# Gated linear attention on Trainium2: loads and weight splits moved ahead around the state scan

## The chip, the core and the metric

The kernel runs on one core of one Trainium2 chip. The metric is the device time of one execution in microseconds, median of several runs. Lower is better.

## What is computed

Two transformer-like blocks on a sequence of 1024 tokens of width 1024 (256 context tokens beside it), all in float32. The change lies in the first block, in its gated linear attention, which runs over the sequence in chunks and in both directions:

```python
def step(S, inp):                       # one chunk of q, k, v and log decay
    b = cumsum(ac)
    S_new = exp(b[-1]) * S + einsum('bhjd,bhjv->bhdv', kc * exp(b[-1] - b), vc)
    scores = einsum('bhid,bhjd,bhijd->bhij', qc, kc, decay)
    o = einsum('bhij,bhjv->bhiv', scores, vc) + einsum('bhid,bhdv->bhiv', qc * exp(b), S)
    return S_new, o
...
oc, s_f, s_b = gla_bidir(qc, kc, vc, laf_c, lab_c, 0, 0, with_output=False)   # context
ox, _, _ = gla_bidir(q, k, v, la_f, la_b, s_f, s_b, True)                     # sequence
```

Beside it the same input projection gives `uB`, of which moving averages over 2, 4, 8 and 16 tokens are taken (`multiscale_pool`), and the gates. All of it is multiplied by weights that the kernel streams from HBM.

## The kernel before, in words

Every weight tile (128 x 1024) is loaded into one of two raw buffers `w_raw`, and GpSimd (POOL) splits it into a high and a low part (`split`, L838: `w_hi` at L840, `w_lo` at L843). TensorE (PE) makes a tile's product as 24 matmuls a unit of 512 tokens: high by high, low by high, high by low (`pe_unit`, L478). POOL may overwrite a split buffer when the tile after its last user has begun (semaphore `w_begun`); PE waits for the split (`w_split`); SyncE (SP) loads the next raw tile when the split before it in that buffer is done (`weight`).

Around the change the program has three stages, separated by the semaphore `phase`, which PE, ScalarE (ACT) and VectorE (DVE) each raise:

- **Chunk preparation** ends with phase 6: decayed keys `kt_d`, values `vt_d`, within-chunk scores `pt_d` and decayed queries `qi_d` of the ten chunks (eight of the sequence, two of the context, numbers `NCX` and `NCX + 1`) are stored to HBM.
- **State scan**, phase 6 to 9. PE alternates a weight tile (T_S to T_S + 9, that is 55 to 64) with eight matmuls `s_products` (L2777) that multiply a chunk's keys and values; DVE updates the state with them (`s_update`, L1983). Steps 0 to 9 run backward over all ten chunks, and their states are stored to `sb_d`; steps 10 and 11 run forward over the two context chunks and have no weight tile of their own. ACT loads each step's keys and values into one of two buffers (`s_load`, L1169 and L1170), when the products two steps earlier are done. Meanwhile POOL and SP work on the moving averages: SP loads the 16 halves of `uB` (`u_load`) and a 2 MB table `inv_sb` (semaphore `tab_in`), POOL averages them (`averages(n)`), SP stores them (`u_store`).
- **Output**, phase 9 to 12. For each of the eight chunks PE makes eight matmuls for the state (L2796) and 72 for the output (L2808 to L2811); SP loads five tiles a chunk (`f_load`: keys, values, scores, queries; `f_load_states`: the backward state), three chunks ahead, into three buffers `F_BUFS`, and between them moves the last averages. ACT copies the outputs, and the pool stage follows after phase 12.

The order of POOL's work in the scan is written out by hand: in step n it splits tile T_S + 1 + n and then makes `averages(n)`, all behind the waits for phase 6 and for the table.

```python
            pool.wait_ge(phase, 6)
            ...
            pool.wait_ge(tab_in, 64)
            ...
            for n in range(16):
                t = T_S + 1 + n
                if t <= T_POOL:
                    pool.wait_ge(w_begun, t)
                    split(t % 2, t + 1, 16 * (t // 2) + 16)
                averages(n)
```

Of the kernel before, what the change touches and what calls it, by code (L numbers as in the profile page):

```python
# [22 lines left out]
P = 128  # L23
# [5 lines left out]
H = 512  # L29
EPS = 1e-6  # L30
HEADS, DK, DV = 4, 128, 256
CH = 128
NC = TA // CH
# [62 lines left out]
def build(nc, modt, modw, cond, crow, cols, mats, tabs, hmask, inv, sgb, xT, ctxT, ctx2T, wall, wup, sgw, bias,  # L96
# [7 lines left out]
    with ctx:  # L104
        def sem(name):
            return ctx.enter_context(nc.semaphore(name))
# [6 lines left out]
        def at(name, shape, offset, dt=F32):  # L113

            n = 4
            for s in shape[1:]:
                n *= s
            n = (n + 31) // 32 * 32
            assert offset % 32 == 0 and offset + n <= nc.sbuf_usable_end, (name, offset + n)
            return nc.alloc_sbuf_tensor_at(name, shape, dt, offset=offset), offset + n  # L120
# [127 lines left out]

        skb, a = at("skb", [P, 2, H], stage_end)
        svt, a = at("svt", [P, 2, 1024], a)  # L250
        stb, a = at("stb", [P, 2, HEADS, DV], a)
        s_end = a


        F_BUFS, U_BUFS = 3, 4
        gla_arena = arena + 33 * 1024
        oall, _ = at("oall", [P, 8, T], gla_arena)
        a = arena + 77 * 1024
        fpt, fqi, fkt, fvt, fsb = [], [], [], [], []
        for n in range(F_BUFS):  # L260
            for tiles_of, shape in ((fpt, [P, HEADS, CH]), (fqi, [P, 2, HEADS, CH]), (fkt, [P, H]),
                                    (fvt, [P, 1024]), (fsb, [P, HEADS, DV])):
                each, a = at(f"f{n}_{len(shape)}_{shape[1]}_{a}", shape, a)
                tiles_of.append(each)
        assert a >= s_end
        stf, _ = at("stf", [P, 2, HEADS, DV], arena + 169 * 1024)
        up, a = at("up", [P, U_BUFS, H + 2 * PAD], a)
        sums, a = at("sums", [P, 2, H + 2 * PAD], a)
# [24 lines left out]
        p_ktr = sem("p_ktr")  # L293
        p_kt = sem("p_kt")
        s_in = [sem("s_in0"), sem("s_in1")]
        s_out = [sem("s_out0"), sem("s_out1")]
        s_mm = sem("s_mm")
        s_upd = sem("s_upd")
# [342 lines left out]
        def _(sp):  # L641
# [109 lines left out]
                sp.dma_start(fqi[n].rearrange("p a h n -> p (a h n)"), qi_d[c]).then_inc(f_in[n], 16)  # L751

            def f_load_states(c):
                n = c % F_BUFS
                sp.dma_start(fsb[n].rearrange("p h n -> p (h n)"), sb_d[c]).then_inc(f_in[n], 16)

# [4 lines left out]
            for s in range(8):  # L761
                weight(T_S + 3 + s)
                u_store(s)
            sp.wait_ge(phase, 9)
            for c in range(F_BUFS):
                f_load(c)
                f_load_states(c)
            for c in range(NCX):
# [68 lines left out]
        def _(pool):  # L837
# [20 lines left out]
            with pool.Fori(1, HALVES) as i:  # L858
                for b in range(2):
                    pool.wait_ge(w_high, i * 2 + (b + 2))  # L860
                    nc.gpsimd.tensor_tensor(w_lo[:, b, :], w_raw[:, b, :], w_hi[:, b, :],
                                            ALU.subtract).then_inc(w_split, 1)
            split_pairs(HALVES, (T_S + 1) // 2)


            pool.wait_ge(phase, 6)
            for n in range(U_BUFS):
# [29 lines left out]
                  .then_inc(u_d, 1)  # L897

            for n in range(16):
                t = T_S + 1 + n  # L900
                if t <= T_POOL:
                    pool.wait_ge(w_begun, t)
                    split(t % 2, t + 1, 16 * (t // 2) + 16)
                averages(n)
            split_pairs(T_POOL // 2 + 1, NT // 2)
            pool.wait_ge(w_begun, NT - 1)
# [33 lines left out]
        def _(act):  # L940
# [244 lines left out]
                    s_step(i * 2 + b, b, i * -2 + (NC - 1 - b), (i * -2 + (NC - 2 - b), 1), i)  # L1185
            s_step(NC - 2, 0, 1, (0, 1), NC // 2 - 1)
            s_step(NC - 1, 1, 0, (NCX, 0), NC // 2 - 1)
            s_step(NC, 0, None, (NCX + 1, 0))
            for b in range(2):
                act.wait_ge(s_out[b], 16 * (NC // 2 + 1))  # L1190
            for b in range(2):
# [1431 lines left out]
        def _(pe):  # L2623
# [146 lines left out]
                p_keys(p)  # L2770
            pe.drain().then_inc(phase, 1)

            def s_products(n, b, loads):
                pe.wait_ge(s_in[b], loads)
                pe.wait_ge(s_upd, n + 1)
                for h in range(HEADS):
                    mm = pe.matmul(g[:, 2 * b + h // 2, DV * (h % 2):DV * (h % 2) + DV],  # L2777
                                   skb[:, b, DK * h:DK * h + DK], svt[:, b, DV * h:DV * h + DV],
                                   start=True, stop=True)
                mm.then_inc(s_mm, 1)  # L2780

            with pe.Fori(0, NC // 2) as i:
                for b in range(2):
                    pe_tile(pe, T_ZA + 3 * NC + b, i, 2, 4)
                    s_products(i * 2 + b, b, i * 32 + 32)
            for b in range(2):
                s_products(NC + b, b, 32 * (NC // 2 + 1))
            end_phase(pe, 3)

            for c in range(NCX):  # L2790
                b, n = c % 2, c % F_BUFS
                pe.wait_ge(f_in[n], 80 * (c // F_BUFS + 1))
                if c >= 2:
                    pe.wait_ge(f_upd, c)
                for h in range(HEADS):
# [7 lines left out]
                for h in range(HEADS):  # L2803
                    for v in range(2):
                        bank = pb[h // 2] if b == 0 else g[:, 4 + h // 2, :]
                        o = bank[:, DV * (h % 2) + CH * v:DV * (h % 2) + CH * v + CH]
                        f = slice(DV * h + CH * v, DV * h + CH * v + CH)
                        pe.matmul(o, fvt[n][:, f], fpt[n][:, h, :], start=True, stop=False)  # L2808
                        pe.matmul(o, stf[:, b, h, CH * v:CH * v + CH], fqi[n][:, 0, h, :], start=False,
                                  stop=False)  # L2810
                        mm = pe.matmul(o, fsb[n][:, h, CH * v:CH * v + CH], fqi[n][:, 1, h, :],  # L2811
                                       start=False, stop=True)
                mm.then_inc(f_omm, 1)
            end_phase(pe, 4)
# [462 lines left out]
```

## Time and profile before

| | |
|---|---|
| runs | 2685.05, 2674.70, 2686.24 us; median 2685.05 us |
| the profiled execution | 2682.14 us, span 2680.4 us |
| granted TensorE clock, mean | 0.962 of full speed |
| busy: PE, DVE, POOL, ACT | 2496.2, 1518.1, 1062.3, 731.1 us |
| state scan (phase 6 to 9) | 704.9 to 852.1 us from the span's start |
| output (first loads to last matmul) | 852.1 to 922 us |

PE is busy for 93% of the span. A change can shorten the run only where it removes idle time of PE, time at the lower clock, or matmuls. The span is read in the order of time: an engine's rows give the start of a group, its length, and in brackets the idle time before it with what ended it.

### The profile page before, as it was taken

To read this page: it belongs to the slowest core of one execution; us is meant where nothing else is said; L and a number is where in the kernel's file an instruction comes from. 1 tells how busy PE (TensorE), PEld (TensorE's weight loads), DVE (VectorE), ACT (ScalarE), POOL (GpSimd) and SP (SyncE) were. 2 spreads that over 40 slices of the span, in tenths; PEclk is the share of its full clock that TensorE was granted. 3 is DMA by queue.
4 is the path that set the end of the run, shared out by engine and by line. 5 is a ranking of instruction groups with operands and counts; after the bars stand their busy time and mean duration, and the time that the engine had idled before them with its cause. 6 is when DMAs were issued, how large, how long until landed. Compare 5 with 4: busy or idle time off the path is not lost.

```text
span 2680.4 us, 33036 instructions
## 1 busy us (share of the span) xinstructions
PE 2496.2 (93%) x12008; PEld 2044.2 (76%) x12008; DVE 1518.1 (57%) x2193; ACT 731.1 (27%) x1244; POOL 1062.3 (40%) x493
## 2 busy tenths in 40 slices
PE   8999999999897979999986999899799999999997
PEld 4888788888686857877774888678578888888885
DVE  5796157877411367446796544475864444444446
ACT  4411334444200254223232444342211111111112
POOL 2344333443465524457541111024554444444444
PEclk9999999999898989999997799989899999999998
DMA  9576455444566842434311222421211111111111
GB/s 354 184 256 242 151 162 162 139 157 142 193 226 220 310 145 81 140 102 142 107 42 60 71 77 74 150 88 61 64 55 48 48 47 47 47 47 47 47 47 71
DMA packets 131233, 325.25 MB, mean 121 GB/s; under 512 B 11568, under 2 KB 59248, under 8 KB 125616
## 3 DMA queue, kind: packets, MB, share of 16 engines
q1 hardware_dynamic: 91232, 215.63, 24.4%
q10 hardware_dynamic: 39888, 108.08, 11.4%
q8 instruction: 74, 1.21, 0.2%
q14 instruction: 39, 0.32, 0.0%
HBM read 248.57 MB, written 70.39 MB: 119 GB/s over the span
## 4 chain that ended last, share of the span: by engine, by line
PE 50%; DVE 8%; issue 3%; ACT 1%; DMA 1%; POOL 0%; DVEq 0%; SPq 0%; POOLq 0%; ACTq 0%
PE pb L478 36%; PE g L2979 6%; PE g L3052 2%; PE pb L2979 1%; DVE zcs L2249 1%; PE g L3032 1%; PE g L2960 1%; DVE f_spare L2458 1%; PE g L2839 1%; DMA kept_in<-cs_d 1%; PE g L2958 0%; DVE ml L2465 0%; DVE xl L2161 0%; DVE hl L2528 0%; DVE cb L2507 0%
## 5 line engine op out<-in xcount | busy, mean ns | idle before, releaser
L840 POOL TENSOR_TENSOR w_hi<-w_raw,one 128x1024 fp32r<-128x1024 f32 x191 | 402.3, 2106 | 1450.4 <-PE pb L478 1051.7
L843 POOL TENSOR_TENSOR w_lo<-w_raw,w_hi 128x1024 fp32r<-128x1024 f32 x191 | 517.4, 2709 | 15.0
L478 PE MATMUL pb<-xh,w_hi 128*128 128x512 f32 (+1 forms) x1224 | 476.3, 389 | 30.8 <-POOL w_lo L843 12.9
L478 PE MATMUL pb<-xh,w_lo 128*128 128x512 f32 (+1 forms) x1224 | 468.1, 382 | 0.0
L478 PE MATMUL pb<-xl,w_hi 128*128 128x512 f32 (+1 forms) x1224 | 467.9, 382 | 0.0
L478 PEld LDWEIGHTS pb<-xh,w_hi 128*128 128x128 f32 x1224 | 233.7, 191 | 79.6 <-POOL w_lo L843 14.1
L478 PE MATMUL pb<-mh,w_hi 128*128 128x512 f32 x704 | 279.1, 397 | 15.9 <-DVE ml L2465 7.3
L478 PE MATMUL pb<-mh,w_lo 128*128 128x512 f32 x704 | 276.4, 393 | 0.0
L478 PE MATMUL pb<-ml,w_hi 128*128 128x512 f32 x704 | 276.1, 392 | 0.0
L478 PEld LDWEIGHTS pb<-xl,w_hi 128*128 128x128 f32 x1224 | 233.2, 190 | 44.5
L478 PEld LDWEIGHTS pb<-xh,w_lo 128*128 128x128 f32 x1224 | 233.9, 191 | 42.9 <-issue 0.7
L478 PEld LDWEIGHTS pb<-mh,w_hi 128*128 128x128 f32 x704 | 133.5, 190 | 50.2 <-ACT mh L1605 11.7
L2551 DVE SCALAR_TENSOR_TENSOR x<-pb,modx,x 128x512 f32<-128x512 f32 x160 | 119.1, 749 | 89.1 <-PE pb L478 89.1
L478 PEld LDWEIGHTS pb<-ml,w_hi 128*128 128x128 f32 x704 | 133.7, 190 | 28.3
L478 PEld LDWEIGHTS pb<-mh,w_lo 128*128 128x128 f32 x704 | 133.9, 190 | 27.7 <-issue 0.5
L2505 DVE TENSOR_SCALAR cb<-gp,col 128x1024 f32<-128x1024 f32 x22 | 43.7, 1984 | 189.9 <-ACT gp L1645 187.4
L478 PE MATMUL pb<-hh,w_hi 128*128 128x512 f32 x352 | 138.8, 394 | 12.3 <-DVE x L2551 11.3
L478 PE MATMUL pb<-hl,w_hi 128*128 128x512 f32 x352 | 137.1, 389 | 0.0
L478 PE MATMUL pb<-hh,w_lo 128*128 128x512 f32 x352 | 137.1, 389 | 0.0
L1645 ACT ACTIVATE gp<-pb 128x512 f32<-128x512 f32 x40 | 24.0, 599 | 375.7 <-PE pb L478 375.7
L973 ACT ACTIVATE stage<-pb 128x512 f32<-128x512 f32 x80 | 47.5, 595 | 279.8 <-PE pb L478 261.3
L478 PE MATMUL pb<-bh,w_hi 128*128 128x512 f32 x256 | 102.7, 401 | 8.4 <-DVE bl L2108 4.7
(410 smaller groups left out, 4635.1 us busy)
## 6 DMA issues: line engine op xcount, KB each, us to landing
w_raw<-in_wall SPq DMA_DIRECT2D x190, 512.0 KB, 3.6
mod_later<-in_modw SPq DMA_DIRECT2D x28, 1024.0 KB, 6.4
proj_d<-stage ACTq DMA_DIRECT2D x40, 512.0 KB, 2.7
at_bias<-in_bias SPq DMA_DIRECT2D x64, 192.0 KB, 2.5
mod_raw<-in_modt SPq DMA_DIRECT2D x8, 1024.0 KB, 11.0
w_raw<-in_wall ACTq DMA_DIRECT2D x15, 512.0 KB, 7.0
svt<-vt_d ACTq DMA_DIRECT2D x12, 512.0 KB, 4.8
vc<-proj_d SPq DMA_DIRECT2D x10, 512.0 KB, 6.1
```

What stands on the lines that cost most here:

```text
L478: mm = pe.matmul(pb[bank][:, 0:n], w[:, b, wc:wc + P], x[:, k, tokens], start=(count == 0), stop=(count == total - 1))
L840: nc.gpsimd.tensor_tensor(w_hi[:, b, :], w_raw[:, b, :], one[:, 0:1].to_broadcast([P, 1024]), ALU.mult).then_inc(w_high, 1)
L843: nc.gpsimd.tensor_tensor(w_lo[:, b, :], w_raw[:, b, :], w_hi[:, b, :], ALU.subtract).then_inc(w_split, 1)
L973: act.activation(rows[:, b, lo:hi], pb[u % 2][:, 0:hi - lo], ACT.Copy, scale=scale)\
L2249: nc.vector.scalar_tensor_tensor(zcs[:, t, :], hpad[:, t, bass.ds(tap, T)], col[:, bass.ds(tap + (cw + TAPS * t), 1)], zcs[:, t, :], ALU.m ...
L2458: nc.vector.scalar_tensor_tensor(f_spare[:, 4 + k % 3, :], x2[:, k, half_of(n)], gain[:, 0, k:k + 1], f_spare[:, 2 + n, :], ALU.mult, ALU. ...
L2505: v = nc.vector.tensor_scalar(cb[:, kt, :], gp[:, kt, 0:T], w, None, ALU.mult)
L2551: nc.vector.scalar_tensor_tensor(x2[:, m, half], pb[u % 2][:, :], modx[:, 64 + m:65 + m], x2[:, m, half], ALU.mult, ALU.add).then_inc(bank ...
L2839: mm = pe.matmul(g[:, u, :], mean_v, osq[:, v, H * u:H * u + H], start=(v == 0), stop=(v == 1))
L2960: pe.matmul(g[:, s % 2, 0:HL], low, local(keys[rows, :]), start=False, stop=True)
L2979: mm = pe.matmul(dst[:, 0:n], w[:, t0 % 2, at_k:at_k + P], x[:, k, tokens], start=(begun and k == kts[0] and w is w_hi and x is xhi), stop ...
L3052: mm = pe.matmul(g[:, 4, 64 * j:64 * j + 64], ptr[:, s % 2, P * c:P * c + P], v, start=(c == 0), stop=(c == 4))
```

## The change

1. POOL splits tile T_S + 1 before it waits for phase 6, and from then on is one tile ahead: in step n of the averages it splits T_S + 2 + n.
2. The last scan step's keys and values get buffers of their own (`skx`, `svx`, semaphore `s_last`). SP loads them after the fourth store of averages in the scan; ACT's `s_step(NC, ...)`, which loaded them, is removed.
3. At the same place SP loads four of the five tiles of the first output chunk. The fifth, the backward state, is not loaded: PE reads it from the scan's own buffer `stb[:, 1]`, and waits for 64 counts instead of 80 on that buffer's semaphore. At phase 9 SP loads two chunks instead of three.
4. The tiles move in SBUF so that output buffer 0 and `skx`, `svx` share no space with the scan's.

```diff
-        stb, a = at("stb", [P, 2, HEADS, DV], a)
+        stb, a = at("stb", [P, 2, HEADS, DV], a + 3 * 1024)
...
-        a = arena + 77 * 1024
+        a = s_end
         for n in range(F_BUFS):
+            if n == 1:
+                f_end, a = a, arena + 77 * 1024
...
+        skx, a = at("skx", [P, H], f_end)
+        svx, a = at("svx", [P, 1024], a)
...
             def f_load_states(c):
+                if c == 0:
+                    return
...
             for s in range(8):
                 weight(T_S + 3 + s)
                 u_store(s)
+                if s == 3:
+                    sp.dma_start(skx[:, :], kt_d[NCX + 1][:, 0:H]).then_inc(s_last, 16)
+                    sp.dma_start(svx[:, :], vt_d[NCX + 1]).then_inc(s_last, 16)
+                    f_load(0)
             sp.wait_ge(phase, 9)
-            for c in range(F_BUFS):
+            for c in range(1, F_BUFS):
                 f_load(c)
                 f_load_states(c)
...
+            def split_next(t):
+                pool.wait_ge(w_begun, t)
+                split(t % 2, t + 1, 16 * (t // 2) + 16)
+
             split_pairs(HALVES, (T_S + 1) // 2)
-
+            split_next(T_S + 1)
 
             pool.wait_ge(phase, 6)
...
             for n in range(16):
-                t = T_S + 1 + n
-                if t <= T_POOL:
-                    pool.wait_ge(w_begun, t)
-                    split(t % 2, t + 1, 16 * (t // 2) + 16)
+                if T_S + 2 + n <= T_POOL:
+                    split_next(T_S + 2 + n)
                 averages(n)
...
-            s_step(NC, 0, None, (NCX + 1, 0))
...
-            for b in range(2):
-                s_products(NC + b, b, 32 * (NC // 2 + 1))
+            pe.wait_ge(s_in[0], 32 * (NC // 2 + 1))
+            s_products(NC, 0, skb[:, 0], svt[:, 0])
+            pe.wait_ge(s_last, 32)
+            s_products(NC + 1, 1, skx, svx)
             end_phase(pe, 3)
...
-                pe.wait_ge(f_in[n], 80 * (c // F_BUFS + 1))
+                pe.wait_ge(f_in[n], 80 * (c // F_BUFS + 1) - (16 if n == 0 else 0))
...
-                        mm = pe.matmul(o, fsb[n][:, h, CH * v:CH * v + CH], fqi[n][:, 1, h, :],
+                        before = fsb[n] if c else stb[:, 1]
+                        mm = pe.matmul(o, before[:, h, CH * v:CH * v + CH], fqi[n][:, 1, h, :],
```

How the order on two engines changes. On POOL, at the start of the scan, before (`up` are the buffers of the averages, `sums` their partial sums; the first split here is tile 56):

```order
L869 MEMSET up 128x8 [waits phase]
L869 MEMSET up 128x8 x3
L840 TENSOR_TENSOR w_hi<-w_raw,one 128x1024 [waits w_begun,w_in0,tab_in,u_s]
L843 TENSOR_TENSOR w_lo<-w_raw,w_hi 128x1024 [waits w_high]
L887 TENSOR_TENSOR sums<-up 128x527 [waits u_d,u_in0]
L894 TENSOR_TENSOR sums<-sums,inv_sb 128x512 [waits u_s]
L896 TENSOR_TENSOR up<-sums,up 128x512 [waits u_s]
L840 TENSOR_TENSOR w_hi<-w_raw,one 128x1024 [waits w_in1,w_begun]
L843 TENSOR_TENSOR w_lo<-w_raw,w_hi 128x1024 [waits w_high]
```

and with the change:

```order
L851 TENSOR_TENSOR w_hi<-w_raw,one 128x1024 [waits w_in0,w_begun]
L854 TENSOR_TENSOR w_lo<-w_raw,w_hi 128x1024 [waits w_high]
L884 MEMSET up 128x8 [waits phase]
L884 MEMSET up 128x8 x3
L851 TENSOR_TENSOR w_hi<-w_raw,one 128x1024 [waits w_begun,w_in1,tab_in,u_s]
L854 TENSOR_TENSOR w_lo<-w_raw,w_hi 128x1024 [waits w_high]
L902 TENSOR_TENSOR sums<-up 128x527 [waits u_d,u_in0]
L909 TENSOR_TENSOR sums<-sums,inv_sb 128x512 [waits u_s]
L911 TENSOR_TENSOR up<-sums,up 128x512 [waits u_s]
```

The split of tile 56 now stands in front of the wait for the phase, and the split that waits for the table (`tab_in`) is that of tile 57.

On SP, in the middle of the scan with the change (before, the row of the second `w_raw` followed directly on the first `up`):

```order
L739 DMA d_d<-up 128x512 [waits u_d]
L733 DMA up<-proj_d 128x520 [waits u_out2]
L772 DMA skx<-kt_d 128x512
L773 DMA svx<-vt_d 128x1024
L753 DMA f_2_512_167616_114<-kt_d 128x512
L754 DMA f_2_1024_169664_115<-vt_d 128x1024
L755 DMA f_3_4_161472_112<-pt_d 128x512
L756 DMA f_4_2_163520_113<-qi_d 128x1024
L682 DMA w_raw<-in_wall 128x1024 [waits w_split]
L739 DMA d_d<-up 128x512 [waits u_d]
```

Six loads (`f_...` are output buffer 0's tiles) are put between the fourth store of averages and the load of weight tile 62, and the five loads that stood first behind the wait for phase 9 are gone from there.

## Rows read from the trace of the kernel before

**Rows 1.** The page's first line: the span.

```profile
span 2680.4 us, 33036 instructions
```

**Rows 2.** Waits of PE from 690 to 930: us, times, longest.

```profile
PE pb L478 <- POOL w_lo L843: 12.0, 1, 12.0
PE g L2796 <- DMA f<-sb_d: 12.0, 1, 12.0
```

**Rows 3.** POOL in order of time: start, us, operation, idle before.

```profile
704.96 0.21 POOL L869 MEMSET up<- 128x8 f32 x4 [12.66 <-ACTq L459]
720.77 1.89 POOL L840 TENSOR_TENSOR w_hi<-w_raw,one 128x1024 fp32r<-128x1024 f32 x1 [15.60 <-issue]
722.74 2.34 POOL L843 TENSOR_TENSOR w_lo<-w_raw,w_hi 128x1024 fp32r<-128x1024 f32 x1
```

**Rows 4.** PE in the scan, in order of time.

```profile
699.69 0.49 PE L478 MATMUL pb<-xh,w_hi 128*128 128x512 f32 x1 [0.44 <-issue]
711.10 1.99 PE L2777 MATMUL g<-svt,skb 128*128 128x256 f32 x8 [0.23 <-DMA svt<-vt_d]
725.13 0.79 PE L478 MATMUL pb<-xh,w_hi 128*128 128x512 f32 x1 [12.04 <-POOL w_lo L843]
740.30 0.58 PE L478 MATMUL pb<-xh,w_hi 128*128 128x512 f32 x1
803.40 0.58 PE L478 MATMUL pb<-xh,w_hi 128*128 128x512 f32 x1
814.48 1.89 PE L2777 MATMUL g<-svt,skb 128*128 128x256 f32 x8
816.02 0.58 PE L478 MATMUL pb<-xh,w_hi 128*128 128x512 f32 x1
```

**Rows 5.** DMA issues from 706.5 to 707.5: count, KB each, median us to landing.

```profile
inv_sb<-in_inv SPq DMA_DIRECT2D x1, 2048.0 KB, 13.9
svt<-vt_d ACTq DMA_DIRECT2D x1, 512.0 KB, 12.3
```

**Rows 6.** PE at the scan's end and in the output stage.

```profile
839.72 3.61 PE L2777 MATMUL g<-svt,skb 128*128 128x256 f32 x16
846.65 3.68 PE L2777 MATMUL g<-svt,skb 128*128 128x256 f32 x8 [3.32 <-DMA svt<-vt_d]
862.31 3.75 PE L2796 MATMUL g<-f,f 128*128 128x256 f32 x8 [11.97 <-DMA f<-sb_d]
871.87 1.89 PE L2796 MATMUL g<-f,f 128*128 128x256 f32 x8
914.39 1.89 PE L2796 MATMUL g<-f,f 128*128 128x256 f32 x8
```

**Rows 7.** DVE's state updates of scan steps 9 and 11.

```profile
841.88 1.66 DVE L1983 SCALAR_TENSOR_TENSOR stb<-stb,dec,g 128x256 f32<-128x256 f32 x4 [10.93 <-PE g L2777]
...
850.37 1.66 DVE L1983 SCALAR_TENSOR_TENSOR stf<-stf,dec,g 128x256 f32<-128x256 f32 x4 [5.07 <-PE g L2777]
```

**Rows 8.** SP's queue: the first load behind phase 9, and two state loads.

```profile
852.11 0.33 SPq L748 DMA_DIRECT2D f<-kt_d  x1
...
854.07 0.55 SPq L755 DMA_DIRECT2D f<-sb_d  x1
...
902.23 0.47 SPq L755 DMA_DIRECT2D f<-sb_d  x1
```

**Rows 9.** Those two state loads' landing (issues 853.5 to 854.6, then 902 to 902.6).

```profile
f<-sb_d SPq DMA_DIRECT2D x1, 512.0 KB, 8.1
...
f<-sb_d SPq DMA_DIRECT2D x1, 512.0 KB, 11.2
```

**Rows 10.** Stretches: length, busy PE, PEld, DVE, ACT, POOL, then PEclk, DMA share, GB/s.

```profile
753.00:766.00 13.00, 13.00 (x60) 10.84 (x59) 1.65 (x4) 1.20 (x2) 7.89 (x5) 1.00 0.68 229
...
857.00:872.00 15.00, 9.69 (x57) 9.00 (x58) 1.65 (x4) 0.00 (x0) 0.00 (x0) 0.66 1.03 404
872.00:900.00 28.00, 28.00 (x224) 27.17 (x223) 6.63 (x16) 4.34 (x8) 19.46 (x17) 1.00 1.02 379
```

More of the change, by code:

```diff
@@ L264, in build @@
                 tiles_of.append(each)
-        assert a >= s_end
+        assert a <= s_end - 4096
+        skx, a = at("skx", [P, H], f_end)
+        svx, a = at("svx", [P, 1024], a)
         stf, _ = at("stf", [P, 2, HEADS, DV], arena + 169 * 1024)
@@ L295, in build @@
         s_in = [sem("s_in0"), sem("s_in1")]
+        s_last = sem("s_last")
         s_out = [sem("s_out0"), sem("s_out1")]
@@ L2771, in _, with s_products @@
             pe.drain().then_inc(phase, 1)
-            def s_products(n, b, loads):
-                pe.wait_ge(s_in[b], loads)
+            def s_products(n, b, keys, values):
                 pe.wait_ge(s_upd, n + 1)
@@ L2777, in s_products @@
                     mm = pe.matmul(g[:, 2 * b + h // 2, DV * (h % 2):DV * (h % 2) + DV],
-                                   skb[:, b, DK * h:DK * h + DK], svt[:, b, DV * h:DV * h + DV],
+                                   keys[:, DK * h:DK * h + DK], values[:, DV * h:DV * h + DV],
                                    start=True, stop=True)
@@ L2784, in _ @@
                     pe_tile(pe, T_ZA + 3 * NC + b, i, 2, 4)
-                    s_products(i * 2 + b, b, i * 32 + 32)
-            for b in range(2):
-                s_products(NC + b, b, 32 * (NC // 2 + 1))
+                    pe.wait_ge(s_in[b], i * 32 + 32)
+                    s_products(i * 2 + b, b, skb[:, b], svt[:, b])
+            pe.wait_ge(s_in[0], 32 * (NC // 2 + 1))
+            s_products(NC, 0, skb[:, 0], svt[:, 0])
+            pe.wait_ge(s_last, 32)
+            s_products(NC + 1, 1, skx, svx)
             end_phase(pe, 3)
```

## The prediction, made before the changed kernel was run

> **What bounds the kernel now.** I read the waits of PE first, over the stretch around the scan [rows 2]. Two stand out, 12.0 us each: one for a weight split by POOL (`w_lo`), one for the load of a backward state (`sb_d`). Everything after the output stage follows from PE's end there, so what PE gains before phase 12 moves the rest of the span [rows 1] forward by as much, unless another engine becomes late.
>
> The first wait: PE ends its products at about 712.6 and begins tile 56 at 725.13, after 12.04 us idle [rows 4]. The split it waited for ran on POOL from 720.77 to 725.08 (722.74 + 2.34), and POOL had stood still for 15.60 us before it, though phase 6 was over at 704.96 [rows 3]. The trace names no releaser. The DMA rows do: the averaging table, issued at the phase, took 13.9 us to land [rows 5], which ends at POOL's start. The split needs nothing of that table; it only stands behind the wait for it.
>
> The second: PE's last products of the scan wait 3.32 us for their values, and the first output chunk (c0) waits 11.97 us [rows 6]; its loads go out only behind phase 9, at 852.11, and its last tile, issued at 854.07, landed 8.1 us later, at 862.2 [rows 8, 9].
>
> Both waits also cost clock. Tile 56 and its products took 15.17 us (725.13 to 740.30) against 12.62 in the steady scan (803.40 to 816.02) [rows 4]; chunk c0 took 9.56 us (862.31 to 871.87) against 7.09, the mean of the next six (871.87 to 914.39) [rows 6]. The first eight output-stage matmuls took 3.75 us instead of 1.89 [rows 6]: half speed, the 1.2 GHz level, after a long idle.
>
> **Part 1: the split in front of the phase.** Tile 55 begins at 699.69 and its first matmul takes 0.49 us [rows 4]. POOL's split takes 4.31 us (720.77 to 725.08) [rows 3], so the split of tile 56 now ends near 704.5, before phase 6, and PE does not wait for it. Tile 56 then begins 1.54 us after the products (814.48 to 816.02 in the steady scan), at 711.10 + 1.54 = 712.64. The tile takes 11.08 (803.40 to 814.48) and the products 1.54, so tile 57 is due at 725.26. Its split is the one that now waits for the table: 720.77 to 725.08, ready 0.18 us before it is due. Before, tile 57 began at 740.30 [rows 4]. **Gain 15.0 us**, which is 12.5 of waiting and 2.5 of clock. From tile 58 on POOL has a split and one set of averages in each PE step. It was busy 7.89 us in a 13 us stretch [rows 10], some 3.6 of it averages; were these twice as long, as they grow with the window, split and averages would still fit a step of 12.62. The second pair of keys and values is now needed at 723.7; its values landed 12.3 us after an issue at 706.7 [rows 5], at 719, in time.
>
> **Part 2: the last scan step.** With its values already there, step 11 needs only the state of step 9, ready at 841.88 + 1.66 = 843.54 [rows 7]. Its products take 1.89 us at full clock, its update 1.66, so DVE ends near 847.1 instead of 850.37 + 1.66 = 852.03, and phase 9 falls at 847.2 instead of 852.1. **Gain 4.9 us** at the phase. ACT loses two DMA issues there and waits for nothing new.
>
> **Part 3: the first output chunk.** c0 can start at 847.2 in the time of the old trace, right at the phase. But c1's five loads now are the first behind the phase, as c0's were, and they land at 862.2 - 4.9 = 857.3. So c0 is covered by c1's loads whether it takes 7.09 or 9.56 us, and c1 is what is late next, by up to 3 us. From c1 on there are two bounds for the start of c7:
>
> - PE alone: 857.3 + 6 x 7.09 = 899.8; if c1 starts at the low clock again, 2.5 more, 902.3.
> - The loads. From 857 the DMA share is 1.03 and later 1.02, at 404 and 379 GB/s [rows 10]: the output stage is already full of transfers. The last tile of c7 landed at 902.23 + 11.2 = 913.4 [rows 8, 9], 1 us before c7 began (914.39 [rows 6]). The change takes c0's five tiles out of this stretch, 2.1 MB by their shapes, 5.2 us at 404 GB/s, and starts it 4.9 us earlier: 913.4 - 4.9 - 5.2 = 903.3.
>
> The later bound holds: c7 begins at 903.3 instead of 914.39. **Gain of parts 2 and 3 together 11.1 us**, not the 14.6 that PE alone would give.
>
> **What is moved onto the scan.** Six loads, 2.36 MB, now go out on SP's queue in front of weight tile 62. That stretch runs at 229 GB/s with a DMA share of 0.68, against 404 when full [rows 10]; 175 GB/s to spare carries them and the 0.52 MB weight tile in 16.5 us. PE begins tile 62 at 803.40 - 15.0 = 788.4 and tile 59 three steps earlier, at 750.5; POOL then splits (4.3) and makes the fourth averages (3.6), up to 758.5 or so, so SP issues the weight tile by about 763 after six issues of half a microsecond (0.33 to 0.55 in [rows 8]), and it lands by 779.5 at the latest. The split takes 4.3, so the tile is due at 784. I cost this at nothing; the cover is 4.5 us. ACT's scan loads are issued two steps, 25 us, ahead; even the 12.3 us of [rows 5] fits. What is left, the SBUF moves and the other buffer for `before`, adds no instruction.
>
> **Sum.** 15.0 + 11.1 = 26.1 us off the profiled execution's 2682.14: 2656.0 us. That execution lies 2.9 us under the median of the runs and inside their spread of 2674.7 to 2686.2.
>
> **Rivals.**
>
> *The wait moves one tile on.* Tile 57's margin is 0.18 us. Weight tile 58 is now issued right behind the table, 18 us earlier than before, into a full queue. If its 0.52 MB shared time with the table, the split would be 1.3 us late (at 404 GB/s), and the clock might fall once more, 2.5: 3.8 us, 2660. The far bound is the whole old wait again, 15.0 us, 2671. Against it: c0's tiles landed first though two more chunks were queued behind them, so one queue serves nearly in order. Chance 0.13.
>
> *PE alone sets the output stage.* If the transfers keep up, c7 starts at 899.8: 3.5 us more gain, 2652.5. For it: chunks c1 to c7 showed no wait before. Against it: c7's last tile was only 1 us early. Chance 0.12.
>
> *Every chunk starts at the low clock.* With loads pacing the output stage PE would stand still for part of a microsecond to 3 us before each chunk. A wait of 3.32 us sufficed for the low level: eight products took 3.68 us instead of 1.89 [rows 6]. If all of c1 to c6 took c0's 9.56 us, c7 would start at 857.3 + 57.4 = 914.7, and only part 1 would be left: 2667.4. The Trainium skill, "TensorE: Matmul & The Clock Gate", section "HAM oscillation — how this bites in real kernels", speaks for this: it reports a kernel whose short bursts between DMA waits were throttled anew at every burst. By that rule the sum would be 14.7 instead of 26.1 us. Against it: PE's 0.44 us of idle in front of tile 55 left no trace, 0.49 us for the first matmul [rows 4], and a chunk that takes 9.56 us gives the loads time to catch up, which ends the waits. Chance 0.07.
>
> *Slower: the loads amid the scan hold up weight tile 62.* The place is SP's queue, the price is PE idle from 788.4 until the tile is split. It decides only from a delay of 4.5 us cover plus 26.1 us gain for no change, and of 44 us for a loss of 0.5% (13.4 us, about what a measurement of this kernel can tell from no change); the queue would have to move the 2.9 MB at under 50 GB/s, and [rows 10] shows 229 beside everything else. Chance 0.03.
>
> That a gain of this size is given back later, where no row points, keeps 0.05.
>
> **How the numbers follow.** Forecast 0.60, then 0.12, 0.13, 0.07, 0.03 and 0.05. Faster by over 0.5% means under 2668.7: the forecast, PE alone, most of the moved wait (0.11) and half of the clock case (0.04) give 0.87. Same: the rest of these two (0.05) and the last case, 0.10. Slower 0.03. The range goes from PE alone less the spread of the runs below the profile (7.4): 2645, up to the clock case, 2667.4, with a little spread, 2669.
>
> **What would show it.** POOL has a split ending just before its first `up` memset, then one at the table's landing; PE has no 12 us wait in the scan, and tile 57 starts 14 us after the first products. No wait for `svt` at the scan's end; the first `f` loads 5 us earlier relative to PE; c0 begins without a DMA wait and c1 shows one of up to 3 us. I am wrong in part 1 if PE waits at tile 57 for `w_lo`, in part 3 if c7 starts under 54 us or over 58 us after phase 9, and altogether if tile 62 waits.

## The result, and the profile after

The changed kernel took **2656.33 us** (median of 5 runs, 2648.01 to 2659.43) against 2675.87 us before (median of 5, among them the three shown above): a ratio of **0.9907, 95% interval 0.9887 to 0.9928**. Measured once more, with more runs of both, it was 0.9916 (0.9895 to 0.9937). The forecast of 2656.0 us and its range of 2645 to 2669 hold the time. The profiled execution took 2659.43 us, 22.7 us less than that of before (2682.14).

The page of the changed kernel: PE's busy time is 2.9 us less than before; 22.8 us of span [rows 1] are gone, so most of it is idle time of PE.

```profile
span 2657.6 us, 33035 instructions
## 1 busy us (share of the span) xinstructions
PE 2493.3 (94%) x12008; PEld 2042.5 (77%) x12008; DVE 1516.2 (57%) x2193; ACT 731.2 (28%) x1244; POOL 1057.7 (40%) x493
```

Waits of PE from 690 to 930 (us in total, times, longest). Both waits of 12.0 us [rows 2] are gone. In their place stand 3.3 us for a backward state, now that of the second output chunk (c1), and small ones. (Two more entries of the list, 5.1 us for DVE's `dl` and 3.0 us for its `tick`, lie behind the output stage and are in both kernels.)

```profile
...
PE g L2810 <- DMA f<-sb_d: 3.3, 1, 3.3
...
PE g L2810 <- DVEq L464: 1.8, 1, 1.8
PE g L2788 <- DMA svt<-vt_d: 1.0, 1, 1.0
```

POOL around phase 6 (start, length, operation, idle before; answers to [rows 3]):

```profile
703.83 1.90 POOL L851 TENSOR_TENSOR w_hi<-w_raw,one 128x1024 fp32r<-128x1024 f32 x1 [7.96 <-PE pb L483]
705.80 2.39 POOL L854 TENSOR_TENSOR w_lo<-w_raw,w_hi 128x1024 fp32r<-128x1024 f32 x1
709.14 0.21 POOL L884 MEMSET up<- 128x8 f32 x4 [0.95 <-ACTq L464]
724.78 1.90 POOL L851 TENSOR_TENSOR w_hi<-w_raw,one 128x1024 fp32r<-128x1024 f32 x1 [15.42 <-DMA inv_sb<-in_inv]
726.75 2.38 POOL L854 TENSOR_TENSOR w_lo<-w_raw,w_hi 128x1024 fp32r<-128x1024 f32 x1
```

The split of tile 56 runs in front of the memsets, and the pause of 15.4 us stands between it and the split of tile 57. The releaser that the old trace did not name is named here: the averaging table.

PE in the scan (answers to [rows 4]), then at its end and in the output stage (to [rows 6]):

```profile
703.25 0.49 PE L483 MATMUL pb<-xh,w_hi 128*128 128x512 f32 x1 [0.44 <-issue]
715.46 1.99 PE L2788 MATMUL g<-svt,skb 128*128 128x256 f32 x8 [1.04 <-DMA svt<-vt_d]
728.21 1.89 PE L2788 MATMUL g<-svt,skb 128*128 128x256 f32 x8
740.83 1.89 PE L2788 MATMUL g<-svt,skb 128*128 128x256 f32 x8
...
816.55 1.89 PE L2788 MATMUL g<-svt,skb 128*128 128x256 f32 x8
...
833.12 1.97 PE L2788 MATMUL g<-svx,skx 128*128 128x256 f32 x8 [0.34 <-DVE stb L1995]
836.89 1.99 PE L2810 MATMUL g<-f,f 128*128 128x256 f32 x8 [1.80 <-DVEq L464]
847.55 3.45 PE L2810 MATMUL g<-f,f 128*128 128x256 f32 x8 [3.31 <-DMA f<-sb_d]
856.41 1.89 PE L2810 MATMUL g<-f,f 128*128 128x256 f32 x8
...
891.85 1.89 PE L2810 MATMUL g<-f,f 128*128 128x256 f32 x8
```

Tiles 55 to 58 go by without a wait for POOL: the second and third products stand 12.62 us apart (740.83 - 728.21), the steady step. The last products use `svx`, `skx` and wait 0.34 us, for DVE. c0 starts at once behind phase 9, and c1 shows the 3.31 us, with the low clock behind it: 3.45 us for eight matmuls, then 8.86 us for the chunk (847.55 to 856.41) against 7.09 (856.41 to 891.85, five chunks).

The stretches (length, busy PE, PEld, DVE, ACT, POOL, then PEclk, DMA share, GB/s; to [rows 10]): the scan with the moved loads, and the output stage cut where the clock changes. The 56 matmuls of c0's 7.30 us are 8 for the state and 48 for the output, not the 72 of the description above.

```profile
764.00:777.00 13.00, 13.00 (x59) 10.84 (x58) 1.66 (x4) 1.20 (x2) 8.42 (x6) 1.00 0.94 318
...
836.90:844.20 7.30, 7.30 (x56) 6.94 (x56) 1.66 (x4) 0.00 (x0) 4.40 (x4) 1.00 0.84 304
844.20:849.10 4.90, 1.59 (x6) 1.26 (x6) 0.00 (x0) 1.09 (x2) 0.00 (x0) 0.88 1.03 408
849.10:852.00 2.90, 2.90 (x14) 2.54 (x13) 0.96 (x3) 0.00 (x0) 0.00 (x0) 0.61 1.03 388
...
872.00:892.00 20.00, 20.00 (x164) 19.54 (x163) 4.97 (x12) 2.17 (x4) 18.19 (x16) 1.00 1.03 408
```

In these stretches of the output stage the DMA share was under 1 only in c0's time. SP's queue and the last state's landing (to [rows 8, 9]): phase 9 falls at 836.87, c7's state is issued at 879.71 and lands 11.7 us later, at 891.4, 0.4 us before c7 begins.

```profile
836.87 0.33 SPq L753 DMA_DIRECT2D f<-kt_d  x1
...
879.71 0.43 SPq L762 DMA_DIRECT2D f<-sb_d  x1
```

```profile
f<-sb_d SPq DMA_DIRECT2D x1, 512.0 KB, 11.7
```

### The profile page after: what moved, and what is told of

Same layout as the page of the kernel before. It is cut to its first block, busy times and chain, and to the rows that moved or that the text cites. A ratio compares the mean times of both kernels' runs of the same rounds, so it can differ in the third digit from the quotient of the medians.

```text
span 2657.6 us, 33035 instructions
## 1 busy us (share of the span) xinstructions
PE 2493.3 (94%) x12008; PEld 2042.5 (77%) x12008; DVE 1516.2 (57%) x2193; ACT 731.2 (28%) x1244; POOL 1057.7 (40%) x493
## 3 DMA queue, kind: packets, MB, share of 16 engines
q1 hardware_dynamic: 91376, 215.90, 24.9%
## 4 chain that ended last, share of the span: by engine, by line
PE 50%; DVE 8%; issue 3%; ACT 1%; DMA 1%; DVEq 0%; POOL 0%; SPq 0%; ACTq 0%
PE pb L483 36%; PE g L2994 6%; PE g L3067 2%; PE pb L2994 1%; DVE zcs L2261 1%; PE g L3047 1%; PE g L2975 1%; DVE f_spare L2470 1%; PE g L2854 1%; DVE xl L2173 1%; DMA kept_in<-cs_d 1%; PE g L2973 0%; DVE ml L2477 0%; DVE hl L2540 0%; DVE cb L2519 0%
## 5 line engine op out<-in xcount | busy, mean ns | idle before, releaser
L854 POOL TENSOR_TENSOR w_lo<-w_raw,w_hi 128x1024 fp32r<-128x1024 f32 x191 | 516.2, 2703 | 14.9
L483 PEld LDWEIGHTS pb<-mh,w_hi 128*128 128x128 f32 x704 | 133.5, 190 | 50.3 <-ACT mh L1617 11.7
```

Of the source, the lines that this page charges most:

```text
L483: mm = pe.matmul(pb[bank][:, 0:n], w[:, b, wc:wc + P], x[:, k, tokens], start=(count == 0), stop=(count == total - 1))
```

## Where the time went, stretch by stretch

Single executions reach tile 55 between 699.7 and 703.4 us, whichever kernel it is, so I cut each trace at six marks: tile 55's start; the third and the ninth products of the scan (the first follow tile 55, the second tile 56, the third tile 57); phase 9 (the first load behind it); c7's first matmul; the end. Differences of starts, us, for both kernels twice (the second profiles are runs e9 and e10 below) and for the experiments:

| kernel | tile 55 at | to 3rd products | to 9th | to phase 9 | to c7 | to the end | tile 55 to c7 |
|---|---|---|---|---|---|---|---|
| before | 699.69 | 51.69 | 75.72 | 25.01 | 62.28 | 1766.0 | 214.7 |
| before, e9 | 701.97 | 51.45 | 75.72 | 24.80 | 62.46 | 1755.9 | 214.4 |
| changed | 703.25 | 37.58 | 75.72 | 20.32 | 54.98 | 1765.8 | 188.6 |
| changed, e10 | 699.81 | 37.93 | 75.72 | 20.32 | 56.11 | 1753.1 | 190.1 |
| e1, splits only | 702.62 | 37.23 | 75.72 | 24.93 | 61.66 | 1765.3 | 199.5 |
| e2, loads only | 702.46 | 50.74 | 75.72 | 20.31 | 54.90 | 1753.0 | 201.7 |
| e3, last step only | 701.97 | 50.48 | 75.72 | 20.31 | 62.45 | 1755.8 | 209.0 |
| e4, table's wait moved | 702.35 | 40.39 | 75.72 | 23.74 | 61.72 | 1755.3 | 201.6 |
| e5, gates late | 702.19 | 36.98 | 75.72 | 20.31 | 55.25 | 1766.5 | 188.3 |
| e6, more bytes | 703.42 | 36.84 | 75.72 | 20.31 | 62.69 | 1768.1 | 195.6 |
| e7, second chunk | 702.51 | 37.40 | 75.72 | 20.31 | 49.79 | 1753.5 | 183.2 |
| e8, all three | 703.19 | 36.84 | 75.72 | 20.31 | 51.63 | 1756.2 | 184.5 |
| e11, e7 and the table | 701.57 | 37.68 | 75.72 | 20.31 | 49.73 | 1756.3 | 183.4 |

Each part of the change acts in one column and leaves the others as they were within 1.1 us (e1 to e3), which is how far single profiles can be trusted here. The column "to the end" falls into two groups some 10 us apart; the kernel before is in both, and so is the changed one. The last section shows where that is. It is why medians of few runs differ by several us from what the columns say.

## The experiments

**e1: the splits alone.** The kernel before with POOL's new order:

```diff
+            def split_next(t):
+                pool.wait_ge(w_begun, t)
+                split(t % 2, t + 1, 16 * (t // 2) + 16)
             split_pairs(HALVES, (T_S + 1) // 2)
+            split_next(T_S + 1)
...
-                t = T_S + 1 + n
-                if t <= T_POOL:
-                    pool.wait_ge(w_begun, t)
-                    split(t % 2, t + 1, 16 * (t // 2) + 16)
+                if T_S + 2 + n <= T_POOL:
+                    split_next(T_S + 2 + n)
```

> The kernel before, with POOL's new order of splits as the only edit. Our theory (the two parts of the change are separate and add up): the 12.0 us for which TensorE waited on w_lo ahead of tile 57 are gone, tile 58 begins about 39 us after tile 55 (before 53.2), the scan's end and the first output chunk stay as they were (10.2 us from the ninth update to phase 9, about 10 us of wait for the chunk's loads), and the run is 14 to 15 us under the kernel before. Rival (given back at the scan's end, because what follows is paced by loads or by DVE): the wait goes but the run is within 3 us of the kernel before.

Ratio 0.9939 (0.9920 to 0.9957), which is 16.3 us of 2679.74; the medians differ by 14.5. The gain lies in the first column (51.6 to 37.2, 14.3 us); phase 9 and the output stage kept their lengths within 0.8 us, so nothing was given back there. Tile 58 follows the third products by 1.54 us, at 38.8 us after tile 55, as our theory had it.

**e2: the loads alone.** The changed kernel with POOL's order as it was (e1's edit undone).

> The changed kernel with POOL's order of splits as it was. Our theory: the 12 us wait for w_lo ahead of tile 57 stands, the scan's end and the output stage are as in the changed kernel (chunk 7 begins about 55 us after phase 9, before 62.3; phase 9 comes 4.7 us sooner after the ninth update), and the run is 11 to 12 us under the kernel before. Rival (the loads amid the scan are only free because the scan's end moved): a wait appears in the scan or in chunk 0, and the gain is under 8 us.

Ratio 0.9949 (0.9931 to 0.9966), which is 13.7 us; the medians differ by 16.7. Tile 55 to c7 is 12.9 us shorter than before, a little over the 11 to 12: 4.6 at phase 9 and 7.5 in the output stage, and 0.8 ahead of the third products, where the loads do nothing. PE in order of time, with the old wait still there and c1's wait of the same size as in the changed kernel:

```profile
728.14 0.80 PE L483 MATMUL pb<-xh,w_hi 128*128 128x512 f32 x1 [12.07 <-POOL w_lo L854]
...
859.86 2.79 PE L2808 MATMUL g<-f,f 128*128 128x256 f32 x8 [3.25 <-DMA f<-sb_d]
```

e1 and e2 together save 27.9 us by the last column, both at once 24.5 and 26.0 (against the mean of the two profiles of before), which is 1.9 to 3.4 us less than the sum. Part of that is spread, since columns that an edit does not act on differ by up to 1.1 us.

**e3: the last scan step alone.** The kernel before with `skx`, `svx`:

```diff
...
                 if s == 3:
+                    sp.dma_start(skx[:, :], kt_d[NCX + 1][:, 0:H]).then_inc(s_last, 16)
+                    sp.dma_start(svx[:, :], vt_d[NCX + 1]).then_inc(s_last, 16)
...
-            s_step(NC, 0, None, (NCX + 1, 0))
...
+            pe.wait_ge(s_last, 32)
+            s_products(NC + 1, 1, skx, svx)
```

> The kernel before, with the tenth step's keys and values loaded into space of their own amid the scan as the only edit; the first output chunk is loaded after phase 9 as it was. Our theory: phase 9 comes 4.7 to 4.9 us sooner after the ninth update, everything after it keeps its length (62.3 us from phase 9 to chunk 7), and the run is 4.7 to 4.9 us under the kernel before. Rival (the loads of the output stage set the end, and what is gained at the scan's end is lost waiting for them): under 2 us.

Ratio 0.9985 (0.9966 to 1.0004); 10 runs do not resolve 5 us of 2680. The trace does: phase 9 comes 4.6 us sooner after the ninth products (20.31 against 24.9), and the output stage keeps its 62.45 us. c0 still waits for its own loads:

```profile
844.75 1.97 PE L2781 MATMUL g<-svx,skx 128*128 128x256 f32 x8 [0.34 <-DVE stb L1988]
858.85 3.75 PE L2803 MATMUL g<-f,f 128*128 128x256 f32 x8 [12.14 <-DMA f<-sb_d]
```

**e4: only POOL's wait for the table, moved behind the first split.**

```diff
-            pool.wait_ge(tab_in, 64)
...
+                if n == 0:
+                    pool.wait_ge(tab_in, 64)
                 averages(n)
```

> The kernel before, in which POOL's wait for the inverse table stands behind the first split and no longer ahead of it; the splits keep their old places otherwise. Our theory (the 15.6 us for which POOL did nothing before its first split were the wait for that table, which landed 13.9 us after its issue): POOL splits tile 56's pair right after its memsets, at 8 to 10 us after tile 55, TensorE does not wait for w_lo ahead of tile 57, and the run is about 15 us under the kernel before, as with the split moved in front of the phase. Rival (something else held POOL, the phase or the weight tile's landing): POOL still begins the split 20 us or more after tile 55, and the time is within 2 us of the kernel before.

Ratio 0.9940 (0.9920 to 0.9960). POOL (first fence) splits right behind its memsets, 5.9 us after tile 55 and sooner than the 8 to 10 us expected, so nothing but the table had held it; the averages now wait for the table:

```profile
707.92 0.21 POOL L869 MEMSET up<- 128x8 f32 x4 [12.96 <-ACTq L459]
708.22 1.89 POOL L840 TENSOR_TENSOR w_hi<-w_raw,one 128x1024 fp32r<-128x1024 f32 x1
710.19 2.39 POOL L843 TENSOR_TENSOR w_lo<-w_raw,w_hi 128x1024 fp32r<-128x1024 f32 x1
723.51 1.06 POOL L886 TENSOR_TENSOR sums<-up 128x527 f32<-128x527 f32 x1 [10.93 <-DMA inv_sb<-in_inv]
...
727.29 1.89 POOL L840 TENSOR_TENSOR w_hi<-w_raw,one 128x1024 fp32r<-128x1024 f32 x1
```

```profile
731.74 0.49 PE L478 MATMUL pb<-xh,w_hi 128*128 128x512 f32 x1 [2.95 <-POOL w_lo L843]
```

One thing I missed: the next split, of tile 57, stands behind the table **and** the first averages, so PE waited 2.95 us for it. The first column gained 11.2 us of e1's 14.3, and tile 55 to c7 13.0 us; the ratio says more (16 us), probably because its six times lie within 4.4 us of its profile's, which is of the shorter group of the last column. That the splits are one step ahead, and not only in front of the phase, is worth those 3 us.

**e5: the gates' loads late.** The changed kernel; ACT issues the two `zb` loads after chunk 5's eviction:

```diff
-            for grp in range(2):
-                act.dma_start(zb[:, grp, :], proj_d[T_ZB + grp][:, 0:T]).then_inc(q_z[grp], 16)
...
+                if c == 5:
+                    for grp in range(2):
+                        act.dma_start(zb[:, grp, :], proj_d[T_ZB + grp][:, 0:T]).then_inc(q_z[grp], 16)
```

> The changed kernel, in which ACT issues its two loads of the gates (1.05 MB together) after it has evicted chunk 5, no longer at the start of the output stage. Our theory (TensorE waited 3.3 us for chunk 1's states because the gates shared the DMA engines with them, at some 404 GB/s for all): chunk 1's states land 2.6 us sooner, TensorE waits about 0.7 us for them, its clock does not fall in chunk 1 (which took 8.86 us against 7.09 for the others), and the run is 3 to 4 us under the changed kernel. Rival (a chunk's loads land when their own issues and latencies let them): the wait stays over 2.5 us and the run is within 1 us of the changed kernel. Second rival (the gates then come too late for the stage behind): the time goes back at the first use of the gates, and the run is no shorter or longer.

Ratio to before 0.9909 (0.9886 to 0.9931), the same as the changed kernel's. The first half of our theory held: c1 waited 1.11 us and kept its clock. The gain did not come. PE's rows:

```profile
843.69 1.99 PE L2811 MATMUL g<-f,f 128*128 128x256 f32 x8 [1.11 <-DMA f<-sb_d]
...
879.35 1.89 PE L2811 MATMUL g<-f,f 128*128 128x256 f32 x8
890.45 2.83 PE L2811 MATMUL g<-f,f 128*128 128x256 f32 x8 [3.85 <-DMA f<-sb_d]
```

The wait came back at c7 (3.85 us), whose state (issued at 875.12 us) now shared the engines with the gates (issued at 879.56; DMA share 1.03 to 1.04 from then on). c7 began 55.25 us after phase 9, where the changed kernel's had 54.98. The bytes up to c7 are the same in both, and so is the time: this is what a bound by loads looks like. Neither rival had the place right.

**e6: more bytes.** The changed kernel with a copy within HBM beside each of chunks 1 to 7:

```diff
+        more_d = dram("more_d", [NCX, P, 1024])
...
+                if c:
+                    sp.dma_start(more_d[c], vt_d[c]).then_inc(f_in[n], 16)
...
-                pe.wait_ge(f_in[n], 80 * (c // F_BUFS + 1) - (16 if n == 0 else 0))
+                pe.wait_ge(f_in[n], 96 * (c // F_BUFS + 1) - (32 if n == 0 else 0))
```

> The changed kernel, in which each of chunks 1 to 7 also copies 0.26 MB from one place of HBM to another (0.52 MB read and written) and waits for that copy with its loads. Our theory (in the output stage the loads nearly bind beside TensorE: chunk 7 began 55.0 us after phase 9, and its states had landed 0.4 us before): chunk 7 begins 62 to 65 us after phase 9, TensorE waits at most of the chunks, and the run is 7 to 10 us over the changed kernel. Rival (the transfers have slack behind chunk 1 and TensorE alone sets the pace): only chunk 1 waits longer, by 1 to 2 us, and the run is 1 to 3 us over the changed kernel.

Each copy was 512 KB, twice what the expectation says of its size. c7 began 62.69 us after phase 9, 7.7 us later, and PE waited at c1, c5, c6 and c7, 9.3 us in all; three of these rows:

```profile
848.33 3.78 PE L2813 MATMUL g<-f,f 128*128 128x256 f32 x8 [4.66 <-DMA f<-sb_d]
...
881.16 1.99 PE L2813 MATMUL g<-f,f 128*128 128x256 f32 x8 [1.52 <-DMA f<-sb_d]
...
898.98 3.78 PE L2813 MATMUL g<-f,f 128*128 128x256 f32 x8 [2.81 <-DMA f<-sb_d]
```

The 3.67 MB cost 7.7 us. At 404 GB/s they take 9.1, of which 1.2 fit the free sixth of c0's 7.3 us: a sum of 7.9, which is an estimate from these rates. The median was 2661.08 us, only 4.8 over the changed kernel's, but of four runs in both groups (2655.8, 2656.9, 2665.3, 2668.8); the profiled executions differ by 9.4.

**e7: the second chunk ahead of phase 9 as well.** The changed kernel; c1's five tiles get space of their own:

```diff
+            sp.wait_ge(unit_done, UNIT[T_POOL])
+            sp.wait_ge(s_out[0], 16 * (NC // 2 + 1))
+            f_load(1)
+            f_load_states(1)
             sp.wait_ge(phase, 9)
-            for c in range(1, F_BUFS):
+            for c in range(2, F_BUFS):
...
+            sp.wait_ge(f_omm, NCX + 1)
             q_load(3)
```

The last wait keeps SP's last load of finished averages (`q_load(3)`) behind chunk 7's matmuls. In the changed kernel that load went out at 895.86 us, 4.0 us behind c7's start, so it takes no bytes out of the time up to c7.

> The changed kernel, in which chunk 1's tiles have space of their own and are loaded before phase 9, when tile 64's products have ended. Our theory (chunk 1's wait of 3.3 us and the 1.8 us for which it then ran longer than the others are all that TensorE loses in the output stage behind chunk 0): both go, chunk 7 begins about 50 us after phase 9, and the run is about 5 us under the changed kernel. Rival (the loads set the stage's pace together with TensorE, so the wait moves to chunk 2 or 3): a wait of 2 us or more appears there and the run gains under 2 us.

**2641.20 us (2639.85 to 2643.61), ratio to before 0.9855 (0.9834 to 0.9877): the fastest kernel of the study.** SP issues c1's loads from 828.44, 7.5 us before phase 9, and PE runs through:

```profile
828.44 0.33 SPq L762 DMA_DIRECT2D f<-kt_d  x1
```

```profile
835.97 1.99 PE L2824 MATMUL g<-f,f 128*128 128x256 f32 x8 [1.80 <-DVEq L473]
843.16 1.89 PE L2824 MATMUL g<-f,f 128*128 128x256 f32 x8
...
885.73 1.99 PE L2824 MATMUL g<-f,f 128*128 128x256 f32 x8
```

Seven chunks in 49.8 us is 7.11 each: PE alone. The changed kernel needed 55.0 and 56.1. Its median is 15 us under the changed kernel's, more than the 5 expected: its profiled execution lies in the shorter group of the last column, and its five times within 4 us. The changed kernel's second profile is of that group too, and there the difference is 3.8 us of time (2641.01 against 2644.80), 6.9 from tile 55 to c7 (5.4 against the first profile).

**e8: e7, e5 and the table's wait behind the split of tile 57.**

> The changed kernel with the second chunk loaded ahead, the gates' loads behind chunk 5's eviction, and POOL's wait for the inverse table behind the split of tile 57's pair. Our theory: chunk 7 begins about 50 us after phase 9, tile 57 waits for nothing (0.5 us in the changed kernel), and the run is 5.5 to 7 us under the changed kernel, which makes it the fastest of all. Rival (the three pieces pay for the same microseconds): no faster than the better of the two single edits.

2643.96 us (2642.66 to 2645.74), ratio 0.9862 (0.9838 to 0.9887): not under e7, so the rival holds. As in e5 the late gates bring a wait at c7, here of 1.7 us: c7 begins 51.63 us after phase 9 instead of 49.79. Tile 57 had nothing to lose, as e11 shows.

**e9 and e10: both kernels again.**

> The kernel before once more, for a second profile of it. Nine kernels with other edits begin tile 55 at 702.0 to 703.4 us, the one profile of the kernel before at 699.7 us. Our theory (the 2 to 4 us are the spread of single executions, since some of those edits touch nothing ahead of tile 55): this profile begins tile 55 between 699.5 and 703.5 us, and from there chunk 7 of the output stage begins 214 to 216 us later (before 214.7). Rival (the kernel before always reaches tile 55 at 699.7 us, and each edit costs some 3 us ahead of it): 699.5 to 700 us again.

> The changed kernel once more, for a second profile and more times on the chip of the runs beside it. Theory: chunk 7 begins 188 to 190 us after tile 55 (188.6 in its first profile), TensorE's clock falls in chunk 1 again, and the times fall into two groups some 8 to 10 us apart, as the stretch behind 1440 us runs at half or full clock. Rival (its longer runs are the spread of a single chip): one group.

Tile 55 began at 701.97 in the kernel before and at 699.81 in the changed one, so this is the spread of single executions, as the theory said. c7 came 214.4 us after tile 55 before, as expected. In the changed kernel it was 190.1, a tenth over the range: c1 took 10.0 us instead of 8.86, again at the low clock:

```profile
844.45 3.78 PE L2810 MATMUL g<-f,f 128*128 128x256 f32 x8 [3.30 <-DMA f<-sb_d]
854.45 1.89 PE L2810 MATMUL g<-f,f 128*128 128x256 f32 x8
```

The times do fall into two groups: the kernel before, 2672.88 to 2675.12 and 2682.83 to 2685.23, five each; the changed kernel, 2644.80 and 2646.12, and 2657.47 to 2659.32 in four, so 10 us apart before and nearer 12 in the changed one.

**e11: e7 and the table's wait alone.**

> The kernel with the second output chunk loaded ahead, and POOL's wait for the inverse table behind the split of tile 57's pair, the gates' loads where the changed kernel has them. Theory: the 0.9 us that the second chunk's kernel loses around tile 57 are gone, chunk 7 begins about 49.8 us after phase 9 without a wait, and the run is 0.5 to 1 us under the kernel with the second chunk alone, 5.5 to 6.5 us under the changed kernel where the clock behind 1440 us is the same. Rival (tile 57's wait was hidden behind the values' landing): no difference from the kernel with the second chunk alone.

2643.07 us (2641.57 to 2649.90), ratio 0.9874 (0.9854 to 0.9894): no difference from e7 that these runs show, and the columns give none (183.4 and 183.2 from tile 55 to c7). The rival holds. The half microsecond that I had counted at tile 57 was not there to be gained: the second and third products of the changed kernel, between which tile 57 lies, are 12.62 us apart (728.21 to 740.83), the steady step. The first and second are 12.75 apart, 0.13 over it.

## Why the prediction was right, and where it was not

**Part 1 (15.0 us).** Mechanism right: POOL's pause was the table (e4), and the split in front of the phase takes PE's wait away (e1). Between the first and the third products the profiled pair gained 14.9 us (40.28 to 25.37). Up to the third products it was 14.1, and 13.5 in the second pair, because the first values landed later: PE waited 1.04 us for them instead of 0.23. The step "tile 56 then begins at 711.10 + 1.54" took the landing of the values as fixed. Whether tile 58's load, which is issued earlier, delays them is not shown: among the kernels with the split moved the same wait ran from 0.3 to 1.4 us, among those without from 0.2 to 0.6.

**The margin at tile 57.** The rival of the moved wait did not come. The split ended at 729.13; the second products began at 728.21 and take 1.54 before the tile can start, so the margin was 0.6 us. The forecast had 0.18; the later first products helped here. How thin it is shows in e4, where the averages in between cost 2.95 us.

**Part 2 (4.9 us).** 4.7 in the profiled pair, 4.5 in the second, 4.6 in e3 by itself.

**Part 3 (6.2 us in the output stage, c7 at 56.1 us after phase 9).** Measured 54.98 and 56.11, a gain of 7.3 and 6.3 us. c1's wait was forecast as up to 3 us and was 3.3. The forecast took the later of two bounds, "the loads: 903.3", and in neither profile did these loads hold c7: its state landed 54.5 us after phase 9 in the first and 55.4 in the second (issued at 877.71, 11.5 us to landing), 0.4 and 0.7 us before c7 began without a wait. What set c7 was PE's own path: 10.7 us to c1's start, its wait of 3.3 us among them, 8.86 for c1 at the low clock, 5 x 7.09, 55.0 in all (56.1 in the second profile, where c1 took 10.0). That is the forecast's other bound, 902.3, which is 55.1 us after phase 9. So the size came out right by some luck: the forecast named the wrong one of two bounds, which lie within 0.4 to 0.7 us of each other. That the loads bind nearly as tightly is shown: e5 moved the wait without shortening the stage, e6 lengthened it by the bytes' time, and e7, which takes c1's tiles out, reached PE's own pace. Relieving PE alone therefore gains nothing, as in e5. The rival of PE alone at full clock (c7 3.5 us sooner) fell in the changed kernel on the 1.8 us that c1 lost at the low clock and on c1's start, 10.7 us after phase 9 where the forecast had 10.1; in e5 it fell on the loads. The transfers behind c0 ran at 388 to 411 GB/s, where the forecast had 379 to 404. The Trainium skill, "Perfetto Trace Analysis", section "Roofline", lets a core that is active alone exceed the 358 GB/s that it gives as a core's share of HBM, up to about 435 GB/s for its 16 DMA engines; the trace agrees as far as it goes, with 408 GB/s at a share of 1.03.

**The clock in every chunk.** Waits for loads did lower the clock here, but not once a chunk: in the changed kernel only c1 lost it. As I read it, the 1.8 us lost there gave the loads the time that later chunks would have waited; no run shows that by itself. e5 lost the clock in c7, e6 in c1 and c7 (4.66 and 2.81 us of wait, each time 3.78 us for eight matmuls). The rival had the support of the Trainium skill, "TensorE: Matmul & The Clock Gate", section "HAM oscillation — how this bites in real kernels", where a kernel is throttled anew at every burst between waits for loads. No run here shows that at each chunk: in the changed kernel one chunk of seven waited for loads and lost the clock, and of the four that waited in e6 two lost it.

**The loads amid the scan (nothing).** The stretch held 0.94 of the DMA engines' time at 318 GB/s, and the six steps from third to ninth products take 75.72 us in all thirteen profiles, with the moved loads or without: no tile waited.

**The sum.** 26.1 us forecast; from tile 55 to c7 the profiled pair gained 26.1, the second pair 24.4. The first agreement is partly luck: part 1 came 0.9 and part 2 0.2 us short, and part 3 1.1 over. The profiled execution itself gained 22.7 us, because it reached tile 55 3.6 us later than that of before, a spread that e9 and e10 show too. That the median is within half a microsecond of the forecast is luck as well: the medians of five runs each differ by 19.5 us, not 26.1, and the changed kernel's eleven runs lie at 2644.8 to 2648.0 (three), 2652.6 (one) and 2656.3 to 2659.4 (seven).

## What to carry to other kernels

A wait in an engine's program holds back everything written behind it, also what has no need of it; when a trace shows a long pause without a releaser, look for a transfer that lands at its end, and put in front of the wait what can run without it. When a stage's transfers already fill its time, moving the first chunk's loads ahead uncovers the second chunk's: compare the bytes up to the last chunk with the time there is, and take bytes out of the stage rather than shift them within it. And cut traces at marks around the edit: parts of 5 us that ten runs of the whole kernel cannot tell from nothing are plain in one profile each.

## What the runs showed of the hardware that was not expected

The same kernel has two lengths, some 10 us apart, mostly by what the clock does in one stretch far behind the change. The kernel before in its first profile, and in its second (e9), for the same 33 us (columns as above):

```profile
1467.00:1500.00 33.00, 31.89 (x136) 28.84 (x136) 21.98 (x42) 9.83 (x29) 4.25 (x2) 0.50 0.23 65
```

```profile
1467.00:1500.00 33.00, 27.84 (x167) 24.23 (x168) 24.54 (x52) 11.71 (x34) 4.25 (x2) 0.85 0.26 72
```

In the first the clock stays at 0.50, the 1.2 GHz level, for all of it, with PE busy 97% of the time; in the second it is mostly at 2.4 GHz, and 31 more matmuls are done. Just ahead of it, in both, PE had waited for ACT, 3.04 and 2.68 us. In the first trace the span's rest behind c7's start is 10.1 us longer (1766.0 against 1755.9): 1.8 us of it arise ahead of that wait's end, and 8.0 in the next hundred microseconds (1466.74 to 1571.99 against 1466.91 to 1564.21 for the same pair of matmuls). Both kernels show both lengths.

One row tells the two apart in all thirteen profiles, that of the `kb,ql` matmul just before the wait; here again the first profile and the second:

```profile
1463.14 0.45 PE L2960 MATMUL g<-kb,ql 64*128 64x384 f32 x1
```

```profile
1463.33 0.68 PE L2960 MATMUL g<-kb,ql 64*128 64x384 f32 x1
```

In the five profiles of the longer kind this matmul took 0.45 us and the wait 3.03 or 3.04. In the eight of the shorter kind it took 0.68 or 0.69, so the clock had already fallen (granted 0.60 around it in the second profile, 1.00 in the first), the wait was 2.54 to 2.68 us, and the matmuls `g<-mat,pr` ran at full speed again 7 us behind its end. In the longer kind they were still slow at 32 us and fast at 40. So in these profiles it is settled before the wait which of the two it will be. What settles it stayed open: no run was made for it. The kernels e4, e7 and e8 showed only times of one group, in 4 to 6 runs each, which may be chance or not.
